# A chunked RWKV recurrence on 64x64 products: half of the head pairs keep their token rows in the other partition half

## The reference

```python
def step(state, inp):
    r_t, w_t, k_t, v_t, kk_t, b_t = inp
    sa = jnp.einsum('bhvk,bhk->bhv', state, -kk_t)
    state = (state * w_t[:, :, None, :] + sa[..., None] * b_t[:, :, None, :]
             + v_t[..., None] * k_t[:, :, None, :])
    return state, jnp.einsum('bhvk,bhk->bhv', state, r_t)
```

## Time and profile before

| | |
|---|---|
| median of 3 runs | 3129.53 us (3128.91 to 3129.88) |
| span of the profiled execution | 3129.4 us |
| TensorE matmuls busy | 2931.8 us, 94% of the span |
| weight loads busy | 1889.1 us, 60% |
| VectorE, ScalarE, GpSimd busy | 1556.1, 957.6, 637.5 us |
| the recurrence | from about 1291 to 1830 us of the span |

### The profile page before, as it was taken

One profiled execution on the slowest core, in us unless ns is written; L12 is line 12 of the kernel. 1 busy time (PEld: TensorE's weight loads), 2 busy tenths in 40 slices (PEclk: granted clock), 3 DMA queues, 4 the chain that ended last, 5 costly groups with the idle time before them and its releaser, 6 DMA issues. The chain is left out here.

```text
span 3129.4 us, 66008 instructions
## 1 busy us (share of the span) xinstructions
PE 2931.8 (94%) x25434; PEld 1889.1 (60%) x25435; DVE 1556.1 (50%) x3592; ACT 957.6 (31%) x2271; POOL 637.5 (20%) x780
## 2 busy tenths in 40 slices
PE   8999999999969999799999989997699999999999
PEld 6778877777746666688888855554233333333333
DVE  4676767677778889433333357775111111111111
ACT  3343334333447777322222223332000000000000
POOL 0000000000035555200000000001233333333333
PEclk9999999999989999899999999998799999999999
DMA  7121111112131000411111113335498878776763
GB/s 241 61 70 62 62 62 63 61 58 73 61 104 41 28 15 1 142 37 45 45 45 37 37 55 108 108 95 202 126 328 295 301 273 320 281 272 251 254 238 120
DMA packets 190197, 397.46 MB, mean 127 GB/s; under 512 B 16155, under 2 KB 76443, under 8 KB 188913
## 3 DMA queue, kind: packets, MB, share of 16 engines
q1 hardware_dynamic: 169440, 343.47, 31.7%
q0 software_dynamic: 20512, 50.54, 4.7%
HBM read 327.25 MB, written 80.32 MB: 130 GB/s over the span
## 5 line engine op out<-in xcount | busy, mean ns | idle before, releaser
L325 PE MATMUL pj_big<-pj_xnT,pj_w_in 128*128 128x256 f32 x2816 | 634.8, 381 | 4.6 <-ACT pj_ubuf L397 3.0
L325 PEld LDWEIGHTS pj_big<-pj_xnT,pj_w_in 128*128 128x128 f32 x2816 | 537.4, 191 | 85.7 <-ACT pj_ubuf L397 6.9
L1810 PE MATMUL ex_pgu<-keep_res,ex_xT 128*64 128x512 f32 x2560 | 568.9, 597 | 0.0
L1810 PEld LDWEIGHTS ex_pgu<-keep_res,ex_xT 128*64 128x64 f32 x2560 | 177.1, 137 | 334.9 <-issue 334.9
L1918 DVE TENSOR_TENSOR ex_hh<-ex_sg,ex_pgu 128x256 f32<-128x256 f32 x80 | 33.7, 421 | 584.0 <-ACT ex_sg L1883 584.0
L1828 PE MATMUL ex_py<-keep_res,ex_hT 128*64 128x512 f32 x1280 | 288.3, 592 | 1.0 <-DVE ex_yb L1926 1.0
L758 POOL TENSOR_SCALAR at_tt<-at_e,at_cf 128x512 f32<-128x512 f32 (+3 forms) x160 | 219.3, 1374 | 185.7 <-DVE at_pd L802 163.5
L1329 PE MATMUL mg_po<-keep_res,mg_mix 128*128 128x512 f32 x512 | 234.1, 614 | 7.0 <-DVE mg_mix L1632 7.0
L737 ACT ACTIVATE at_e<-at_sc,at_nmx 128x512 f32<-128x512 f32 (+3 forms) x320 | 196.9, 623 | 68.9 <-DVE at_nmx L780 66.6
L295 POOL TENSOR_TENSOR pj_m<-pj_qn,pj_cosin 128x256 f32<-128x256 f32 x64 | 46.6, 728 | 827.6 <-DVE pj_qn L524 601.4
L1883 ACT ACTIVATE ex_sg<-ex_pgu 128x256 f32<-128x256 f32 x80 | 30.7, 384 | 582.5 <-PE ex_pgu L1810 582.5
(11 more groups left out here) (293 smaller groups left out, 4720.1 us busy)
## 6 DMA issues: line engine op xcount, KB each, us to landing
keep_res<-in_w_exp_gate SPq DMA_DIRECT2D x32, 2048.0 KB, 8.6
keep_res<-in_w_exp_up SPq DMA_DIRECT2D x32, 2048.0 KB, 15.5
keep_res<-in_w_exp_down SPq DMA_DIRECT2D x32, 2048.0 KB, 8.6
chunks_s<-pj_st SPq DMA_DIRECT2D x32, 642.0 KB, 4.0
rw_raw<-chunks_s SPq DMA_DIRECT2D x32, 642.0 KB, 3.9
pj_xt<-in_x SPq DMA_DIRECT2D x20, 512.0 KB, 3.8
qk_s<-pj_qo SPq DMA_DIRECT2D x64, 128.0 KB, 1.9
mg_xin<-in_x SPq DMA_DIRECT2D x8, 1024.0 KB, 7.1
```

What stands on the lines that cost most here:

```text
L325: ins = pe.matmul(out, lhs, rhs, start=(k == 0), stop=(k == KC - 1))
L1810: ins = pe.matmul(pgu[j * BT:(j + 1) * BT, :, :], lhs, wgu[x][:, k, :, j * HE:(j + 1) * HE], start=(k == 0), stop=(k == KC - 1))
```

## The change

The head pairs 2 and 3 now keep everything that has token rows in the other partition half: for them, what is read from feature rows `r` is written to token rows `1-r`. Their feature-token products so use the two quarters off the diagonal. `every` takes pairs `j` and `j + 2` together, so that four products in a row name four quarters; for token-token products the same order names the token halves 0, 1, 1, 0. The eight one-bank PSUM tiles become four of two banks each (`F`, `G`, `H`, `W`; pairs 0, 1 in the first bank, 2, 3 in the second), with `G` and `H` changing places each turn. The group `s1` is parted: its `gk`-by-values half becomes a group of its own, `s0`, which is issued between `gl` and `gb`, waits for VectorE's mask of `gk` only, and closes with a semaphore; `s1` (8 products) and `y2` wait on TensorE's own semaphore, for `s0` and `y1`. The number of products stays 216 in a turn.

```diff
-SERIAL = ("s1", "s2", "s3", "y1", "y2", "y3")
-PE_ORDER = ("gl", "gb", "s1", "r1", ...
+SERIAL = ("s0", "s1", "s2", "s3", "y1", "y2", "y3")
+PE_ORDER = ("gl", "s0", "gb", "s1", "r1", ...
...
-        ps = [m.ps(f"ps{n}", [P, 512]) for n in range(8)]
+        ps = [m.ps(f"ps{n}", [P, NPAIR, 4 * C]) for n in range(4)]
...
         def quarter(n, k=0):
-            return ps[n][:, 256 * k:256 * k + 256].rearrange("p (a n) -> p a n", n=C)
+            return ps[n][:, :, k * C:(k + 1) * C]
+        def pairs(n):
+            return ps[n][:, :, 0:2 * C]
+
+        def turned(c, has_serial):
+            n = c + 1 if has_serial else 0
+            return (1, 2) if n % 2 == 0 else (2, 1)
...
+        def token_half(p, r):
+            return HALVES[r] if p < NPAIR // 2 else HALVES[1 - r]
...
-                    for p in range(NPAIR):
+                    for j in range(NPAIR // 2):
                         for f in products:
-                            for rows in HALVES:
-                                ins = f(p, rows)
+                            for p in (j, j + NPAIR // 2):
+                                for r in range(2):
+                                    ins = f(p, HALVES[r], token_half(p, r))
...
-                    every(lambda p, r: product(quarter(1)[r, p, :], cin[nx][r, p, A], cin[nx][r, p, B]))
-                    every(lambda p, r: product(pairs(0)[r, p, :], cin[nx][r, p, B], cin[nx][r, p, AR]), parted=False)
+                    every(lambda p, r, t: product(quarter(F)[t, p, :], cin[nx][r, p, A], cin[nx][r, p, B]))
+                if has_serial:
+                    pe.wait_ge(s_dve, d.before() - 1)
+                    every(lambda p, r, t: product(quarter(H)[t, p, :], gk[x][t, p, 0:C], tv[x][t, p, :],
+                                                  start=p % (NPAIR // 2) == 0, stop=False), parted=has_pre)
+                if has_pre:
+                    every(lambda p, r, t: product(pairs(G)[t, p, :], cin[nx][r, p, B], cin[nx][r, p, AR]), parted=has_serial)
                 if has_serial:
                     pe.wait_ge(s_dve, d.before())
                     pe.wait_ge(s_act, a.before())
-                    every(lambda p, r: product(quarter(2)[r, p, :], cin[x][r, p, A], state[r, p, :], stop=False),
-                          lambda p, r: product(quarter(2)[r, p, :], gk[x][r, p, 0:C], tv[x][r, p, :], start=False))
+                    pe.wait_ge(s_pe, done.after("s0"))
+                    every(lambda p, r, t: product(quarter(H)[t, p, :], cin[x][r, p, A], state[r, p, :],
+                                                  start=False, stop=p % (NPAIR // 2) == 1))
...
-                    every(lambda p, r: product(quarter(3)[r, p, :], tbk[x][r, p, 0, :], sa[r, p, :], stop=False),
-                          lambda p, r: product(quarter(3)[r, p, :], tbk[x][r, p, 1, :], tv[x][r, p, :], start=False))
+                    every(lambda p, r, t: product(quarter(G)[r, p, :], tbk[x][t, p, 0, :], sa[t, p, :], stop=False),
+                          lambda p, r, t: product(quarter(G)[r, p, :], tbk[x][t, p, 1, :], tv[x][t, p, :], start=False))
...
                 if has_serial:
-                    every(lambda p, r: product(quarter(5)[r, p, :], tv[x][r, p, :], gk[x][r, p, C:2 * C], False, False),
+                    pe.wait_ge(s_pe, done.after("y1"))
+                    every(lambda p, r, t: product(quarter(H)[r, p, :], tv[x][t, p, :], gk[x][t, p, C:2 * C], False, False),
                           parted=False)
```

More of the change, by code:

```diff
@@ L810, in _ @@
             ch.end("attend, VectorE")
-SERIAL = ("s1", "s2", "s3", "y1", "y2", "y3")
-PE_ORDER = ("gl", "gb", "s1", "r1", "s2", "r2", "tok", "r3", "s3", "r4", "y1", "r5", "y2", "r6", "y3", "r7", "gk", "r8")
+SERIAL = ("s0", "s1", "s2", "s3", "y1", "y2", "y3")
+PE_ORDER = ("gl", "s0", "gb", "s1", "r1", "s2", "r2", "tok", "r3", "s3", "r4", "y1", "r5", "y2", "r6", "y3", "r7", "gk", "r8")
 ACT_ORDER = ("s1", "r1", "s2", "r2", "tok", "r3", "r5", "y3", "r7")
@@ L915, in half @@
                 d = Pieces(s_dve, DVE_ORDER, c, has_pre, has_serial)
+                done = Pieces(s_pe, PE_ORDER, c, has_pre, has_serial)
                 nx = 1 - x if has_serial else x
+                F, G, H, W = 0, *turned(c, has_serial), 3
                 def product(out, lhs, rhs, start=True, stop=True):
@@ L945, in half @@
                 if has_pre:
                     pe.wait_ge(s_dve, d.after("gb"))
-                    every(lambda p, r: product(pairs(3)[r, p, 0:C], gl[r, p, 0, :], gb[nx][r, p, U]),
-                          lambda p, r: product(pairs(3)[r, p, C:2 * C], gb[nx][r, p, U], gl[r, p, 0, :]))
+                    every(lambda p, r, t: product(quarter(W, 0)[t, p, :], gl[t, p, 0, :], gb[nx][t, p, U]),
+                          lambda p, r, t: product(quarter(W, 1)[t, p, :], gb[nx][t, p, U], gl[t, p, 0, :]))
@@ L949, in half @@
                 if has_serial:
                     pe.wait_ge(s_act, a.after("s1"))
-                    every(lambda p, r: product(quarter(4)[r, p, :], q5[x][r, p, :], sa0[r, p, :]))
+                    every(lambda p, r, t: product(quarter(F)[t, p, :], q5[x][t, p, :], sa0[t, p, :]))
                 if has_pre:
                     pe.wait_ge(s_act, a.after("r1"))
-                    every(lambda p, r: product(pairs(5)[r, p, :], w[r, p, 2, :], w[r, p, 0:2, :].rearrange("p a n -> p (a n)")),
-                          lambda p, r: product(quarter(6)[r, p, :], w[r, p, 1, :], w[r, p, 2, :]))
@@ L956, in half @@
-                    every(lambda p, r: product(pairs(7)[r, p, 0:C], cin[nx][r, p, B], eye[r, :]),
-                          lambda p, r: product(pairs(7)[r, p, C:2 * C], cin[nx][r, p, K], eye[r, :]),
-                          lambda p, r: product(quarter(1)[r, p, :], cin[nx][r, p, V], eye[r, :]), parted=False)
+                    every(lambda p, r, t: product(pairs(G)[t, p, :], w[t, p, 2, :], w[t, p, 0:2, :].rearrange("p a n -> p (a n)")),
+                          lambda p, r, t: product(quarter(H)[t, p, :], w[t, p, 1, :], w[t, p, 2, :]))
@@ L959, in half @@
+                    every(lambda p, r, t: product(quarter(W, 0)[t, p, :], cin[nx][r, p, B], eye[r, :]),
+                          lambda p, r, t: product(quarter(W, 1)[t, p, :], cin[nx][r, p, K], eye[r, :]),
+                          lambda p, r, t: product(quarter(W, 2)[t, p, :], cin[nx][r, p, V], eye[r, :]), parted=False)
                     pe.wait_ge(s_act, a.after("r2"))
                     pe.wait_ge(s_dve, d.after("r2"))
-                    every(lambda p, r: product(quarter(0)[r, p, :], lu4[r, 0, p, :], q[0][r, p, :]),
-                          lambda p, r: product(quarter(2)[r, p, :], lu4[r, 1, p, :], lu4[r, 0, p, :]))
+                    every(lambda p, r, t: product(quarter(F)[t, p, :], lu4[t, 0, p, :], q[0][t, p, :]),
+                          lambda p, r, t: product(quarter(H)[t, p, :], lu4[t, 1, p, :], lu4[t, 0, p, :]))
```

65 lines of the change are left out of this document (33 added, 32 removed).

## The result

The changed kernel takes 3144.64 us (median of 4 runs, 3141.86 to 3146.03); the kernel before took 3129.70 beside it (4 runs, 3128.91 to 3130.97). The ratio is 1.0047, with an interval of 1.0035 to 1.0058: slower by 15 us, where 3114.0 was forecast. The profiled execution took 3146.0, its span 3144.2.

What follows compares the result with a forecast made beforehand. Bound: one chain of products and copies per turn, its slots filled with other products. Slots 13.0 us, first turn 1.2, last 0.9, longer turns 0.4: total 15.5, so 3129.5 - 15.5 = 3114.0 us, range 3109 to 3132 (0.82).

Steps and rivals of the forecast that it cites:

- The rivals that rested on either: Four-quarter groups: weight loads bind at 58 ns a product, 3132, chance 0.08; or a start rate in between, near 3118, 0.10.
- that of the order 0, 1, 1, 0: Token-token groups: the new order leaves one half idle, +100 us, 3230; chance 0.05.
- The sum of the slots: Gain per turn in slots `r2` to `r3` (0.28 us) and `r3` to `r4` (0.14); 13.0 us over 31 turns.
- The ends: First turn, at clock 0.50, gains 0 to 2.5 us, taken 1.2; last turn, without preparation beside it, 0.9.
- the forecast's first range: Whole kernel with full or near full four-quarter overlap: 3109 to 3121 us, chance 0.60.
- of the 5.0 us of longer turns, a part falls into slots with 1.5 us to spare: 0 to 5, taken 0.4: Recurrence: 5.0 us from a few turns longer than 16.32 us; slack would absorb part, gaining 0.4 us.
- The remark that the clock might fall in the longer waits: Recurrence: TensorE's clock falls in longer waits, named within "something slower that I don't name"; chance 0.03, no size.
- two quarters at a time: Rival: only two quarters ever overlap, so `s0` ahead of `gb` delays `r1` 0.50 us a turn; +15.5, 3145, chance 0.07.

Runs made afterwards that it cites:

- e14: Kernel before with 32 useless four-column products more a turn, 16 behind `s1` and 16 behind `y2` (128 instructions more); 3151.7 us, ratio 1.0074.
- e2: Changed kernel on two diagonal quarters only, with half the columns in the products meant for four quarters, from the third chunk on; 31 turns 524.8 us.
- e7: e5 without TensorE's two waits on its own semaphore (for `s0` and `y1`); 3130.3 us, ratio 1.0011.
- e5: Changed kernel with all products kept in the two diagonal quarters and `s0` put behind `gb`; 3136.3 us, ratio 1.0029.
- e6: Changed kernel, four quarters kept, with `s0` put behind `gb`; 3132.6 us, ratio 1.0015.
- e10: Changed kernel with each 642 KB chunk load split into four parts started at different places of the turn; 3133.4 us, ratio 1.0017.
- e12: Kernel before with each chunk load split into four parts; 3127.5 us, ratio 1.0001.
- e8: e6 with an identity block in the chunk, so `gb` and `gk` also bring turned B and K: 16 products fewer a turn; 3134.3 us, ratio 1.0020.
- e9: Changed kernel with `tok`, `s3`, `y1`, `y2`, `y3` cut to one product of each kind from the third chunk on; 31 turns 512.6 us.
- e4: Changed kernel with only one product of 8 left in each of `y1`, `y2`, `y3`; 31 turns 515.5 us.
- e11: e8 with each chunk load split into four parts; 3127.1 us, ratio 1.0001.
- e13: Kernel before with 16 useless four-column products more a turn behind `s1` (64 instructions more); 3141.7 us, ratio 1.0048.

## Why the prediction was wrong

**Right: four quarters at once.** In the clean turn that starts at 1670.48, the timeline of the changed kernel's weight loads has all 48 records of `tok` in one row:

```profile
1677.22 0.83 PEld L930 LDWEIGHTS rw_ps<-rw_eye,rw_cin 64*64 64x64 f32 x48
1678.37 0.34 PEld L930 LDWEIGHTS rw_ps<-rw_q,rw_lu 64*64 64x64 f32 x8 [0.32 <-issue]
```

The row's 0.83 us less the 0.14 of the last record leaves 0.69 for 47 starts, 14.7 ns each and 29 a product, 0.70 for `tok`, as forecast; before it was 1.40. The Trainium skill's rule (TensorE: Matmul & The Clock Gate, Part 3, "The mechanism"), that loads overlap with matmuls in flight only where row groups differ, is not what this row shows: twice as many loads go to each row half in the same time, once both column halves are used. Nor does the same page's floor of about 25 ns from start to start ("Wait — 56ns, not 53.3ns?") bound the starts over four quarters, 14.7 ns apart. What was doubled is a pace of each quarter: on two quarters a product takes 58 ns with 4, 32 or 64 columns (e14, e2, before), so up to 64 it isn't the columns that set it. The rivals that rested on either fall, as does that of the order 0, 1, 1, 0: e7 and before share the turn of 16.33.

**Right: the slots.** `r3` starts 1.18 us after `tok` in the timeline above (1557.58 to 1558.76), behind VectorE's copy, which ends at 1558.65; 1.12 was forecast and 1.40 it was. The mask of `gb` follows that of `gl`. `r1` now waits 1.10 us for VectorE in place of 0.41. The sum of the slots, 0.42 a turn, was measured as 0.46. From the start of `r2` to that of `r3` the turn gained 0.30 and from `r3` to `r4` 0.13, as forecast; `r8` to `r1` gave 0.13 for which nothing was set down, since a four-quarter group starts some 0.07 before the group ahead is through, and the other stretches lost 0.10 together. That the sum came out so near is in that part luck. The ends gave 3.4 - 0.6 = 2.8 us where 2.1 were forecast, but no run shows that these are the change's: 1.2 us of the 3.4 lie ahead of the recurrence, and so do parts of what stands behind it (from the last product of the recurrence to the end of the span, 1301.1 us against 1299.8). The last turn alone, from the last mask to the last product, became 0.76 us shorter, with 0.9 forecast. The low end of the forecast's first range, added up by its own terms, is 3110.6 and not 3109; nothing hangs on it.

**Wrong: the step "of the 5.0 us of longer turns, a part falls into slots with 1.5 us to spare: 0 to 5, taken 0.4".** I took the longer turns as a disturbance of fixed size that more slack would swallow, and never asked what they were. In the earlier trace rows they are only a mean of 16.48 beside a turn of 16.32. They are blocks of instructions that come late (12 stops, 7.7 us, in the kernel before), and their cost was not to shrink from 5.0 to 4.6: it grew to 36.5 us. The account in the span: -14.3 for the chain, +31.8 for this, -2.8 for the ends, together +14.7 of the 14.8. The remark that the clock might fall in the longer waits had a share of 0.03 and no price; it did fall, for 23.9 us. If all the work in these had been TensorE's, it would have cost half of them, 12 us; that is an upper bound, and the 7 us by which the five turns go beyond their own stops are the lower one. The measured 3144.6 lies on the 3145 of the rival "two quarters at a time", and that is chance: VectorE got `gb` in time and all four quarters ran.

What the runs show of the cause: the stops stand where blocks of 256 instructions end, and a block is late because its packet was started late. They are in the kernel before too (12); four quarters alone bring them from 16 to 43 (e5, e6); TensorE's waits on itself cost 6 us (e5, e7), the place of `s0` 8 to 10 (after, e6), the undivided load some 8 (after, e10); these overlap and their sum is no account. The new order, tiles and waits cost 8 us over the kernel before without one four-quarter product (e5, 1.0029), and four quarters on top of them gave back 3.7 (e6): they bring more stops and still gain a little. The whole loss against the kernel before comes from what was rearranged for them. More instructions in a TensorE without waits bring none (e14).

What I conclude from that is a guess, argued and not shown: with TensorE as the slower side, some of its instructions would lie ready when a group ends, the next block would be asked for early, and a block that is a little late would be bridged by what lies ready. In the changed kernel TensorE is done before VectorE and ScalarE at almost every wait; then nothing would lie ready behind the wait, the next block would be asked for later, and each late block would stop the array at once. What speaks for it is that the packet starts later as TensorE's busy share falls, in all 17 traces: 0.95 to 1.47 us into the block before at 92 to 96% (six kernels), 1.48 and 1.65 at 86 and 88%, 1.76 to 2.16 at 71 to 80% (nine). Idle time isn't all of it: before and e12 are both at 92%, with 1.43 and 0.95. The stops go by this and by how long a block lasts: e8 and e9, as idle as the changed kernel or more, ask later still, but their blocks last 4.99 and 6.22 us and not 4.54, and they have 24 and 18 stops. e4 and e11 show that this doesn't settle the number: blocks of about the same length there (5.12 and 5.05), 35 and 18 stops.

**Open.** What the start of a packet is tied to: it comes after the block before is in use, late where TensorE waits, but from 0.5 to 5.5 us into that block in the changed kernel alone. Whether short groups without four quarters would do the same, since e2 didn't make them short. Why `s0`'s place weighs so much more than its clean turn shows. And by what a stop brings the clock down one time and not another.

## What to carry to other kernels

A profile's busiest engine, in slots that end in a wait, gives back only what the chain of copies lets it: here 0.46 of 2.97 us a turn. Before unloading it, compare the shortest turn with the mean: the difference is a cost with a cause of its own (here idle time under "issue", at every 256th instruction), and it can grow when the engine is made to wait more. In a long unrolled stretch of small products, spare the engine's waits on itself where the data allow it, and count a stop of over a microsecond as a risk to the clock as well.

## What the runs showed of the hardware that I had not expected

- Instructions come in packets of 16 KB, 256 instructions, one each 4.8 to 5 us in the recurrence (511 us by 106 and 103), each in 0.9 to 1.7 us. Over 17 traces no block was in use sooner than 1.19 us after landing, and 409 of 417 stops stood at a block's end. A stop lasts up to 2.2 us in the changed kernel, 2.95 in e13.
- The queue of chunk loads, 642 KB in some 4 us, makes such stops dearer: 23.2 us beyond the clean turns without it, 36.5 with it, at 44 and 45 stops.
- After a stop of 1.8 us the granted clock was 0.50 for 6.8 us, though TensorE was 81% busy in the 5 us that followed.
- A product of 64 columns on a quarter takes 58 ns where two quarters run and 29 where four do, weight loads included. With 32 columns (e2) and with 4 (e14) it is 58 ns on two quarters all the same.
- Two waits of TensorE on groups of its own, hidden in a clean turn, cost 6 us together over 31 turns of a kernel with two quarters.
